# One decoder layer in split fp32 on one core: another order of loads, weight sums and form steps around the first and the last product pair of the MLP's first half

## What is computed

```python
x = x + token_mixer(rmsnorm(x, norm1_w)) @ w_out          # gated DeltaNet heads and HGRN2 heads
u = jax.nn.relu(rmsnorm(x, norm2_w) @ w_up)               # (tokens, 8192)
x = x + (u * u) @ w_down                                  # (tokens, 2048)
y = rmsnorm(x, final_norm_w)
```

## Time and profile before

| | |
|---|---|
| runs of the kernel before | 2941.31, 2941.51, 2944.43 us; median 2941.51 |
| profiled execution, its own time | 2940.85 us |
| its span, first to last instruction | 2939.0 us |
| PE busy | 2894.1 us (98%) |
| DVE busy | 2049.7 us (70%) |
| ACT busy | 1147.7 us (39%) |
| POOL busy | 322.3 us (11%) |
| mean granted TensorE clock | 0.995 |

### The profile page before, as it was taken

One profiled execution on the slowest core, in us unless ns is written; L12 is line 12 of the kernel. 1 busy time (PEld: TensorE's weight loads), 2 busy tenths in 40 slices (PEclk: granted clock), 3 DMA queues, 4 the chain that ended last, 5 costly groups with the idle time before them and its releaser, 6 DMA issues. The chain is left out here.

```text
span 2939.0 us, 51590 instructions
## 1 busy us (share of the span) xinstructions
PE 2894.1 (98%) x21560; PEld 2846.7 (97%) x21560; DVE 2049.7 (70%) x2864; ACT 1147.7 (39%) x1440; POOL 322.3 (11%) x473
## 2 busy tenths in 40 slices
PE   9999999999999999999999999999989999999998
PEld 8999999999999999999999999999988999999998
DVE  6566666656565757565677777777767878887885
ACT  4333333333333333333444444444433444444454
POOL 6201111111101010112100000000000000000111
PEclk9999999999999999999999999999999999999999
DMA  8344873333334533444255545545576666666665
GB/s 211 69 88 72 90 74 87 77 86 72 89 75 86 79 80 79 121 139 133 80 144 156 147 135 158 156 135 152 156 228 196 192 192 198 188 194 201 193 192 195
DMA packets 516477, 396.53 MB, mean 135 GB/s; under 512 B 18931, under 2 KB 484197, under 8 KB 516245
## 3 DMA queue, kind: packets, MB, share of 16 engines
q1 hardware_dynamic: 462272, 267.95, 38.8%
q0 software_dynamic: 22672, 88.35, 8.3%
q10 hardware_dynamic: 31300, 36.93, 4.0%
HBM read 308.80 MB, written 84.37 MB: 134 GB/s over the span
## 5 line engine op out<-in xcount | busy, mean ns | idle before, releaser
L989 PE MATMUL main<-h_hi,w_hi 128*128 128x296 f32 (+1 forms) x2592 | 607.5, 315 | 4.9 <-DVE h_lo L1965 2.3
L1354 PE MATMUL main<-forms_a,w_hi 128*128 128x288 f32 x3024 | 605.8, 296 | 5.6 <-DVE w_lo L2547 5.5
L1354 PE MATMUL main<-forms_b,w_hi 128*128 128x288 f32 x3024 | 603.7, 295 | 0.0
L989 PE MATMUL main<-h_lo,w_hi 128*128 128x296 f32 (+1 forms) x2592 | 562.5, 298 | 0.0
L989 PE MATMUL main<-h_hi,w_lo 128*128 128x296 f32 (+1 forms) x2592 | 561.8, 298 | 0.0
L1354 PEld LDWEIGHTS main<-forms_a,w_hi 128*128 128x128 f32 x3024 | 487.1, 189 | 7.2 <-DVE w_lo L2547 7.2
L1354 PEld LDWEIGHTS main<-forms_b,w_hi 128*128 128x128 f32 x3024 | 484.6, 188 | 0.0
L1354 PE MATMUL main<-forms_a,w_lo 128*128 128x288 f32 x1512 | 448.1, 296 | 0.0
L1354 PE MATMUL main<-forms_b,w_lo 128*128 128x288 f32 x1512 | 445.2, 294 | 0.0
L989 PEld LDWEIGHTS main<-h_hi,w_hi 128*128 128x128 f32 x2592 | 413.9, 189 | 18.2 <-issue 10.6
L989 PEld LDWEIGHTS main<-h_hi,w_lo 128*128 128x128 f32 x2592 | 419.9, 188 | 0.0
(11 more groups left out here) (400 smaller groups left out, 3591.3 us busy)
## 6 DMA issues: line engine op xcount, KB each, us to landing
w_raw<-in_w_in SPq DMA_DIRECT2D x128, 512.0 KB, 7.7
w_raw<-in_w_up SPq DMA_DIRECT2D x128, 512.0 KB, 5.0
w_raw<-in_w_down SPq DMA_DIRECT2D x100, 512.0 KB, 6.5
u_forms<-ub POOLq DMA_DIRECT2D x32, 1152.0 KB, 6.2
z<-x_scratch SPq DMA_DIRECT2D x32, 576.0 KB, 6.6
x_scratch<-z POOLq DMA_DIRECT2D x31, 576.0 KB, 6.2
stage<-u_forms ACTq DMA_DIRECT2D x30, 576.0 KB, 3.9
w_raw<-in_w_out SPq DMA_DIRECT2D x32, 512.0 KB, 4.0
```

Source lines behind the costliest of these rows:

```text
L989: ins = mm(out[:, half, :], w[:, ring, k, :], x[:, kx, half * width:half * width + width], start=first and n == 0, stop=last_ and n == 2)
L1354: ins = mm(out, w[:, k, :], x[:, kx, :], start=i in (0, 1, 3) and k == 0 and n == 0, stop=k == KP - 1 and n == 2, skip_group_check=True)
```

## The change

The arithmetic stays the same. What moves is where instructions stand:

- SyncE, before pair 32: the loads of pair 33's blocks 132 and 133 go behind the forms, `load_z(32)` goes ahead of form 4. Block 134 (a11 of pair 33) waits for `weight_sum(32, 3)` instead of r4.
- `weight_sum(32, 3)` writes into `w_sum` (slot 1) and not over a21, and stands at r3's place instead of r1's.
- Pair 33: `mlp_hi` and `mlp_lo` of s0 and s1 and the loads and splits of the step forms stand earlier or later by some places.
- Pair 0: the square sum of the last tile is made by VectorE and not by GpSimd; `token_form(7, 2)`, the halves of m2's and m3's weights and `copy_product(0, 0)` go ahead of other form work; `weight_sum(1, 2)` goes behind `mlp_lo(1, 0)`.

```diff
--- before.py
+++ after.py
@@ -651,7 +651,10 @@
                     elif q != UP_PAIRS:
                         sp.wait_ge(s_lo, split_no(q, 6 if f else 4))
                     if q == UP_PAIRS:
-                        sp.wait_ge(s_unit, unit_of(q, (4, 6, 0, 3)[f]) + 1)
+                        if f:
+                            sp.wait_ge(s_unit, unit_of(q, (4, 6, 0, 3)[f]) + 1)
+                        else:
+                            sp.wait_ge(s_ws, 4 * q + 3)
                 if p < UP_PAIRS:
                     src = w_up[:, j % 2:KT:2, (2 * p + j // 2) * P:(2 * p + j // 2) * P + P]
                 else:
@@ -687,15 +690,16 @@
                 load_block(n)
             load_form(0)
             load_form(1)
-            load_block(first + 4)
-            load_block(first + 5)
             load_block(first + 2)
-            for i in range(2, 5):
-                load_form(i)
+            load_form(2)
+            load_form(3)
+            load_z(UP_PAIRS)
+            load_form(4)
             load_block(first + 3)
             load_form(5)
-            load_z(UP_PAIRS)
+            load_block(first + 4)
             load_form(6)
+            load_block(first + 5)
             for n in range(first + 6, 4 * PAIRS):
                 load_block(n)
                 if n % 4 == 2:
@@ -901,7 +905,7 @@
                 pool.wait_ge(s_sq, m + 1)
                 if m == 0:
                     pool.tensor_copy(sq_sum[:, :], sq[:, 0, :]).then_inc(s_sqs, 1)
-                else:
+                elif m < KT - 1:
                     pool.wait_ge(s_sqs, m)
                     pool.tensor_tensor(sq_sum[:, :], sq_sum[:, :], sq[:, m % 2, :], ALU.add).then_inc(s_sqs, 1)
 
@@ -1327,6 +1331,8 @@
                 out_tile(q, k)
 
             def weight_source(p, i):
+                if i == 4:
+                    return sum_slot(p, 1)
                 return (wblock(block_of(p, {0: 0, 3: 1, 4: 2, 6: 3}[i])) if i in (0, 3, 4, 6)
                         else sum_slot(p, {1: 1, 2: 2, 5: 3}[i]))
 
@@ -1860,7 +1866,9 @@
                     copy_product(p, i - 2)
                 t = p - UP_PAIRS
                 if i < FORMS - 1:
-                    if t:
+                    if t == 1 and i == 0:
+                        step_load(1, 1)
+                    elif t:
                         mlp_hi(p, i + 1)
                 elif p + 1 < PAIRS and t not in (-1, 0):
                     mlp_hi(p + 1, 0)
@@ -1876,12 +1884,11 @@
                         step_load(1, 0)
                     if i == 5:
                         step_hi(1, 0)
+                        mlp_hi(p + 1, 0)
                         chunk_hi(4)
                     if i == 6:
-                        mlp_hi(p + 1, 0)
+                        mlp_hi(p + 1, 1)
                         chunk_hi(5)
-                if t == 1 and i == 1:
-                    step_load(1, 1)
                 if t == 1 and i == 2:
                     step_hi(1, 1)
                     chunk_hi(6)
@@ -1904,11 +1911,11 @@
             mlp_hi(0, 1)
             square(KT - 1)
             form_hi("3b")
+            mlp_hi(0, 2)
             form_hi("2_7")
-            mlp_hi(0, 2)
-            form_hi("4a")
             copy_product(0, 0)
             mlp_hi(0, 3)
+            form_hi("4a")
             copy_product(0, 1)
             form_hi("4b")
             act.wait_ge(s_n2, 1)
@@ -2509,7 +2516,7 @@
                     if p:
                         dve.wait_ge(s_ws, 4 * p - 2)
                         if p == UP_PAIRS + 1:
-                            dve.wait_ge(s_unit, unit_of(UP_PAIRS, 1) + 1)
+                            dve.wait_ge(s_unit, unit_of(UP_PAIRS, 4) + 1)
                         else:
                             dve.wait_ge(s_lo, split_no(p - 1, 1))
                     ins = TT(sum_slot(p, 1), a21, a22, ALU.add)
@@ -2523,7 +2530,11 @@
                     ins = TT(sum_slot(p, 2), sum_slot(p, 1), a11, ALU.subtract)
                 elif n == 3:
                     dve.wait_ge(s_ws, 4 * p + 1)
-                    ins = TT(a21, a11, a21, ALU.subtract)
+                    dst = a21
+                    if p == UP_PAIRS:
+                        dve.wait_ge(s_unit, unit_of(p, 1) + 1)
+                        dst = sum_slot(p, 1)
+                    ins = TT(dst, a11, a21, ALU.subtract)
                 else:
                     loaded(1)
                     dve.wait_ge(s_ws, 4 * p + 2)
@@ -2543,7 +2554,10 @@
                 src = (wblock(block_of(p, {0: 0, 3: 1, 4: 2, 6: 3}[i])) if i in (0, 3, 4, 6)
                        else sum_slot(p, {1: 1, 2: 2, 5: 3}[i]))
                 dve.wait_ge(s_hi, split_no(p, i))
-                dve.wait_ge(s_unit, unit_of(UP_PAIRS, 0) if p == UP_PAIRS + 1 and i < 2 else u_ - 1)
+                if p == UP_PAIRS + 1 and i < 2:
+                    dve.wait_ge(s_unit, unit_of(UP_PAIRS, 0))
+                else:
+                    dve.wait_ge(s_unit, u_ - 1)
                 TT(w_lo[:, u_ % 2], src, hi_slot(u_).bitcast(F32), ALU.subtract).then_inc(s_lo, 1)
 
             def take(p, i):
@@ -2612,7 +2626,7 @@
 
             def raw_step(p, i):
 
-                if i == 1:
+                if i == 3:
                     weight_sum(p, 3)
                 if 2 <= i <= 5:
                     chunk_lo(i - 2, 0)
@@ -2620,6 +2634,7 @@
                 if i == 3:
                     weight_sum(p, 4)
                 if i == 6:
+                    mlp_lo(p + 1, 0)
                     weight_sum(p + 1, 1)
                     step_lo(1, 0)
                     chunk_lo(4, 0)
@@ -2630,7 +2645,7 @@
                     weight_sum(p, 2)
                 if i in (1, 2):
                     chunk_lo(5, i - 1)
-                if i == 2:
+                if i == 3:
                     step_lo(1, 1)
                 if i in (4, 5):
                     chunk_lo(6, i - 4)
@@ -2644,7 +2659,10 @@
                 if t == 0:
                     raw_step(p, i)
                 else:
-                    if (p, i) != (0, 5):
+                    if t == 1 and i < 2:
+                        if i == 0:
+                            mlp_lo(p, 1)
+                    elif (p, i) != (0, 5):
                         mlp_lo(p, i)
                     if t == 1:
                         step_after_raw(p, i)
@@ -2652,9 +2670,12 @@
                         weight_sum(p, 3)
                     if i == 3:
                         weight_sum(p, 4)
+                    if p == 1 and i == 0:
+                        weight_sum(p, 2)
                     if p == 0 or t == -1:
                         if i == 6:
                             weight_sum(p + 1, 1)
+                        if i == 6 and p:
                             weight_sum(p + 1, 2)
                     elif i >= 5 and p + 1 < PAIRS:
                         weight_sum(p + 1, i - 4)
@@ -2676,14 +2697,17 @@
             form_lo("5a")
             mlp_lo(0, 1)
             out_evac(EARLY + KT - 1)
+            token_form(KP - 1, 2)
+            dve.wait_ge(s_sq, KT)
+            dve.wait_ge(s_sqs, KT - 1)
+            TT(sq_sum[:, :], sq_sum[:, :], sq[:, (KT - 1) % 2, :], ALU.add).then_inc(s_sqs, 1)
             form_lo("3b")
-            token_form(KP - 1, 2)
+            mlp_lo(0, 2)
             form_lo("2_7")
             token_form(KP - 1, 3)
             token_form(KP - 1, 4)
-            mlp_lo(0, 2)
+            mlp_lo(0, 3)
             weight_sum(0, 4)
-            mlp_lo(0, 3)
             form_lo("4a")
             form_lo("4b")
             mlp_lo(0, 4)
```

## The result

The changed kernel took 2924.05 us (median of 6 runs, 2923.39 to 2926.99) against 2941.97 of the kernel before in the same session (6 runs, 2940.06 to 2944.53): the medians lie 17.9 us apart, and the ratio of the runs is 0.9944 [0.9934, 0.9955], by which the change is 13 to 19 us faster. The forecast was 2919.0, a gain of 22.5. The profiled execution took 2923.39 us, 17.46 less than that of before.

A forecast was written before the change was run, and what follows sets the result against it. PE is busy 98% of the span, so only two passages' losses, 5.5 and 20.8 us, can be won; 2940.85 - 4.4 - 18.1 = 2918.35, against the median 2919.0 us. Forecast 2916.5 to 2922, range for all 2915.2 to 2928.

The forecast's parts named there:

- rival 1: Second passage: block 134 lands at 2203 instead of 2197.5, s0 waits, DVE's chain ends 5.5 later; 2924.5 us, 16%.
- signs of being wrong: z's issue waits much longer for its store, the step load holds s3, or block 134 lands after 2200.
- First passage: Norm matmuls' end to pair 1's start: loss 5.5 us, new loss 1.1 (0.7 and 0.4), gain 4.4.
- The hold of the copy: First passage: m0, the last x1 store (landing 1460.7) and ACT's queue hold copy_product(0, 0), which ends near 1461.1.
- last-sum move: Pair 0: last square sum on DVE costs some 0.8 us, the 1.12 go, so DVE loses nothing.
- z: Before r2: issued near 2174.9, lands 2177.5 to 2179.5, 3 us to spare; gain 8.0 + 2.1 us.
- s3 and its step load: Pair 33: second step load issued at 2202.2 lands at 2212.8; s3's wait of 5.8 us goes, covered by 1.5.
- Loads behind z: ... 16.4 from 2177.2, so 2193.6: Second passage: loads behind z take 16.4 us at full engines; with pair 31's store, block 134 taken at 2197.5.
- Each form lands 4us or more before its product: Second passage: forms loaded behind z arrive 4 us or more before the raw products that need them.
- The size of the DVE chain: Pair 33, s0's rest to the end of s2's rest: 12.6 us of DVE work, ending at 2211.2.
- the forecast's 2.7: Second passage: new wait of 2.7 us in front of s1 and s2 together, from DVE's chain; gain 18.1.
- the slot of the third sum: weight_sum(32, 3) runs at 2183.2, r4 needs it at 2190.4; its new target costs nothing.

The follow-up runs named there:

- pool_sum: The changed kernel with the last tile's square sum back on GpSimd: 2928.92 us in one run; norm matmuls' end to pair 1's start 17.51 us.
- z_only: The kernel before with only the load of z for pair 32 moved ahead of form 4's load: 2932.65 us, ratio 0.9975.
- blocks_first: The changed kernel with blocks 132 and 133 loaded in their old place ahead of block 130, z still moved: 2918.66 us against 2938.18, ratio 0.9927.
- p2_only: The kernel before with the second passage's edits alone, without those of pair 0 and the square sum: 2928.58 us, ratio 0.9962.
- in_place: The changed kernel with weight_sum(32, 3) written over a21 again and block 134 waiting for r4 as before: 2922.89 us in one run.
- late_store: The changed kernel with pair 31's last two u forms made later by VectorE, behind r4's take, so its store is issued later: 2921.85 us in one run.

## Why the prediction was right and where it failed

- **Where the time fell.** 2924.05 lies in the range for all (2915.2 to 2928), but not in the 2916.5 to 2922 of the forecast itself (61%). It is rival 1's time, 2924.5 (16%), and by rival 1's mechanism. Of the signs of being wrong one came: block 134 landed after 2200.
- **First passage: right.** Loss 5.5, new loss 1.1; measured 0.50 at m4 (forecast 0.7) and 0.42 at pair 1 (0.4), gain 4.0 for 4.4. The hold of the copy was named rightly (the x1 store), but in this execution it began at 1462.28, 0.6 us after the norm matmuls' start, and still in time for m2. That the last-sum move costs DVE nothing was right; pool_sum shows that it wins nothing either.
- **z: right in effect.** Issued in before's coordinates (3.0 added) at 2177.2 and not 2174.9, landed at 2181.9 and not by 2179.5: pair 30's store took 12.6, not 10.2. r2 was due at 2182.7, and the forecast's 3 us to spare took it up. z_only puts this part at 9.0 of the 12.1.
- **s3 and its step load: right in effect, in part by luck.** It landed after 9.7, and s3 did not wait. But it was issued at 2203.75, in before's coordinates 2206.8, and not at 2202.2: on ACT it stands behind the hi half of s1 (started 2203.69), which waits for VectorE and so for block 134. The cover of 1.5 held because s3 was as late.
- **The failed step: "Loads behind z: ... 16.4 from 2177.2, so 2193.6", with block 134 taken at 2197.5.** It landed at 2200.2, in before's coordinates 2203.2: 5.7 late, where rival 1 had put it. The sum of bytes was taken over engines that are always full. The rate in the two holes, 149 and 181 GB/s, against blocks_first's 301 and 397 in the same windows, costs (3 x 152 + 3 x 216) KB = 1.1 MB, 3.0 us at 367 GB/s. Moving blocks 132 and 133 behind the forms made the first hole: nothing was left to transfer while SyncE waited for block 130's slot; p2_only has it too. The second opens where SyncE stands on the store's landing with only z behind it to start the queue again; it is this deep in the profiled execution alone, whose store took 12.6 (346 GB/s in p2_only, and block 134 there 1.6 sooner). From 2176 to 2190 the rate was 344, another 0.9. Of the remaining 1.8 the runs show no split; the store of pair 31 had been counted in full.
- **"Each form lands 4us or more before its product" was right and not enough:** block 131, issued behind the store's landing, was not examined. It landed 10.3 after 2175.07, and r3 waited 1.82.
- **The size of the DVE chain was right,** 2212.55 + 1.22 - 2201.29 = 12.5 for 12.6. So the delay of the block went through to the end in full: s2 started 42.1 after r0's start instead of 2211.2 - 2174.88 = 36.3, and B is 48.64 for 42.7. The waits at s0, s1 and s2, 1.28 + 2.38 + 0.46 = 4.1 for the forecast's 2.7, show only part of it, since r3's wait of 1.8 and the slow s1 (4.95 for 3.35 at a clock of 0.66, which the forecast did not count behind its own new standstill) filled time that TensorE would have stood before s2. They are where TensorE lost the time and not what the end hangs on.
- The forecast gave the slot of the third sum no gain of its own, but called block 134's wait for r4 the cause of s0's 1.5. in_place puts the wait back with all else queued as in the change, and B is the same.

## What to carry to other kernels

When a load is sent ahead, count the stream of transfers with its holes: where one queue issues in order, each wait in it may leave the DMA engines empty, and what the change moved behind that wait is then missing as filler. Put loads whose slots are already free ahead of the first load that has to wait, and then look up for each load behind the moved wait, small ones too, when its reader is due. Find the engine whose chain the last wait hangs on: here every us of block 134 came out at the end, and TensorE's own delays ahead of that wait cost nothing. A new standstill of 2 us may be followed by a slow clock; price it where no later wait takes it up.

## What the hardware showed beyond that

- The rate after a pause: z, alone ahead of a queue that had just run empty, landed 4.7 us after its issue, for 1.6 us of bytes at 367 GB/s; in the full stream of blocks_first it took 7.3. Counted from r0's start it landed at 7.2 and 7.4, though it was issued 2.4 later.
- The slow clock does not follow each standstill of the same size: 2.38 before s1 brought 4.95 for the product in the changed kernel, 2.37 before s1 in p2_only brought 3.44, and there s2, behind 1.96 more, took 4.99. In late_store 1.24 and 1.96 brought none (3.45 and 3.47). What decides was not tested.
- A GpSimd instruction of 1.44 us stretches one VectorE instruction with two inputs from 0.51 to 1.63 or 1.64, in all four kernels that have it there (before, p2_only, z_only, pool_sum); in the changed kernel, which has not, it takes 0.51.
